# Attention values with the value block as the stationary side, SiLU gates from tanh, and weight splits in halves, in a two-layer decoder trunk

## What is computed

```python
h = rmsnorm(x, norm_even[i])
proj = h @ w_in_even[i]
(qa, ka, va, ga, qi, ki, wi, qb, kb, vb, gb, lr) = _split(proj, EVEN_SPLIT)
o_a = dsa_attention(qa, ka, va, qi, ki, wi, rel_bias, top_k)   # top 128 keys of each query
#   logits = einsum('bqhd,bqkhd->bhqk', qa, ks) * scale + bias
#   p = softmax(logits);  return einsum('bhqk,bqkhd->bqhd', p, vs)
o_a = o_a.reshape(B, S, A_W) * jax.nn.silu(ga)
...
o_b = gla(qb, kb, vb, log_a)
o_b = rmsnorm of each head * gla_norm * jax.nn.silu(gb)
x = x + jnp.concatenate([o_a, o_b], axis=-1) @ w_out_even[i]
```

## Time and profile before

| | us |
|---|---|
| median of 3 runs | 527.7 |
| lowest, highest | 527.25, 528.91 |
| the profiled execution | 527.31 |
| its span, first to last instruction | 525.6 |

### The profile page before, as it was taken

One profiled execution on the slowest core, in us unless ns is written; L12 is line 12 of the kernel. 1 busy time (PEld: TensorE's weight loads), 2 busy tenths in 40 slices (PEclk: granted clock), 3 DMA queues, 4 the chain that ended last, 5 costly groups with the idle time before them and its releaser, 6 DMA issues.

```text
span 525.6 us, 7516 instructions
## 1 busy us (share of the span) xinstructions
PE 513.8 (98%) x2807; PEld 414.5 (79%) x2807; DVE 371.1 (71%) x770; ACT 238.8 (45%) x374; POOL 292.3 (56%) x180
## 2 busy tenths in 40 slices
PE   7999999999999999999999999999999999999994
PEld 6866888788888888788888889778777677787883
DVE  3795599669957446466451074999989999869824
ACT  6734743233220434734541445456555554167413
POOL 5470755735634175655333317599999997351701
PEclk9999999999999999999999999999999999999998
DMA  8443363222222002200445303502322222402004
GB/s 267 125 140 120 121 199 122 85 76 81 81 80 82 1 1 80 82 0 1 153 169 153 88 0 120 161 25 81 88 85 75 71 64 89 148 0 82 1 0 160
DMA packets 42386, 46.75 MB, mean 89 GB/s; under 512 B 3176, under 2 KB 30851, under 8 KB 42350
## 3 DMA queue, kind: packets, MB, share of 16 engines
q1 hardware_dynamic: 42350, 46.28, 27.8%
HBM read 44.03 MB, written 2.12 MB: 88 GB/s over the span
## 4 chain that ended last, share of the span: by engine, by line
PE 83%; DVE 10%; ACT 3%; issue 1%; DMA 1%; POOL 1%; SPq 0%; POOLq 0%; ACTq 0%; DVEq 0%
PE bank L1508 31%; PE bank L1528 29%; PE bank L1816 3%; PE bank L1726 3%; PE bank L1653 3%; DVE r_va L1071 2%; PE bank L1703 2%; DVE top L1069 2%; PE bank L1804 2%; PE bank L1715 2%; DVE r_ob L1055 1%; PE bank L1822 1%; PE bank L1544 1%; DMA w_raw<-in_w_in_even_dram 1%; PE bank L1592 1%
## 5 line engine op out<-in xcount | busy, mean ns | idle before, releaser
L536 POOL TENSOR_TENSOR w_lo<-w_raw,w_hi 128x2048 fp32r<-128x2048 f32 (+1 forms) x31 | 140.4, 4531 | 101.8 <-ACT w_hi L683 100.8
L1508 PE MATMUL bank<-hT_hi,w_hi 128*128 128x512 f32 (+1 forms) x280 | 112.9, 403 | 0.0
L1508 PE MATMUL bank<-hT_hi,w_lo 128*128 128x512 f32 (+1 forms) x280 | 110.6, 395 | 0.0
L1508 PE MATMUL bank<-hT_lo,w_hi 128*128 128x512 f32 (+1 forms) x280 | 110.5, 395 | 0.0
L1528 PE MATMUL bank<-w_hi,hT_hi 128*128 128x512 f32 x252 | 102.0, 405 | 0.1
L1528 PE MATMUL bank<-w_hi,hT_lo 128*128 128x512 f32 x252 | 98.4, 391 | 0.0
L1528 PE MATMUL bank<-w_lo,hT_hi 128*128 128x512 f32 x252 | 98.3, 390 | 0.0
L683 ACT ACTIVATE w_hi<-w_raw 128x2048 fp32r<-128x2048 f32 (+1 forms) x35 | 65.6, 1878 | 40.1 <-PE bank L1528 35.3
L1325 DVE SCALAR_TENSOR_TENSOR bank<-r_va,pvec,bank 128x512 f32<-128x512 f32 x108 | 76.0, 749 | 0.9
L616 POOL TENSOR_TENSOR r_g<-r_g 128x512 f32<-128x512 f32 x48 | 62.0, 1293 | 11.4 <-ACT r_g L869 5.7
L1508 PEld LDWEIGHTS bank<-hT_lo,w_hi 128*128 128x128 f32 (+1 forms) x280 | 52.3, 187 | 13.9 <-issue 3.4
(11 more groups left out here) (232 smaller groups left out, 787.6 us busy)
## 6 DMA issues: line engine op xcount, KB each, us to landing
w_raw<-in_w_in_even_dram SPq DMA_DIRECT2D x14, 1024.0 KB, 5.2
w_raw<-in_w_in_odd_dram SPq DMA_DIRECT2D x16, 512.0 KB, 4.6
w_raw<-in_w_out_even_dram SPq DMA_DIRECT2D x4, 1024.0 KB, 7.8
w_raw<-in_w_in_odd_dram SPq DMA_DIRECT2D x4, 1024.0 KB, 5.1
w_raw<-in_w_out_odd_dram SPq DMA_DIRECT2D x4, 1024.0 KB, 5.1
r_x<-in_x_dram SPq DMA_DIRECT2D x4, 512.0 KB, 6.0
r_x<-bias_rows SPq DMA_DIRECT2D x4, 512.0 KB, 6.0
r_x<-in_x_dram SPq DMA_DIRECT2D x1, 2048.0 KB, 8.0
```

What stands on the lines that cost most here:

```text
L536: nc.gpsimd.tensor_tensor(v(w_lo[j % 3]), v(w_raw[j % 2]), v(w_hi[j % 3]).bitcast(F32), ALU.subtract).then_inc(lo_ready, 1)
L1508: ins = nc.tensor.matmul(proj_bank(g)[0:m, :], w[:, k, P * i:P * i + m], h[:, k, :], start=(n == 0), stop=(n == 3 * KC - 1))
```

## The change

- **Values.** `pv_two_heads(p)` serves heads 2p and 2p+1 of step pair p. Now the value block (128 keys x 64) is the stationary side and the transposed probabilities (128 columns) move. The two heads write the lower and the upper 64 partitions of bank 7, so the result comes out transposed, [head pair x 64, query]. It is done at every even step, behind T(n). There are four `probT` buffers instead of two, the new ones in `r_att`.
- **Softmax sums and gates.** `empty_oa` only copies bank 7 to `oaT`. The reciprocal sums are multiplied into the gate rows of ga (`gate_by_sums`), the gate rows are transposed in place of `oa`, and the transposed gate is multiplied by `oaT` in the bank (`gated_transposed`).
- **SiLU** is x/2 (1 + tanh(x/2)): for each bank ScalarE writes x/2 and tanh(x/2) (`half_and_tanh`), VectorE multiplies (`gate_row`, at steps 12, 14, 16, 18 for gb; for ga at 28, 30 and twice behind the last step).
- **Split in halves.** In slots 12 to 15 the high part of slot s+2 is made in two halves, behind `soft(8k+3)` and behind `soft(8k+5)`, and not in one piece ahead of `soft(8k+2)`.

```diff
-        probT = [r_g[:, 2048 + 512 * i:2560 + 512 * i] for i in (0, 1)]
+        probT = [r_g[:, 2048 + 512 * i:2560 + 512 * i] for i in (0, 1)] + \
+            [r_att[:, 512 * i:512 * i + 512] for i in (0, 1)]
+        tanh_row = [r_att[:, 1024 + 512 * i:1536 + 512 * i] for i in (0, 1)]
+        oaT = r_oa[:].rearrange("p (c t) -> p c t", c=4)
...
+            def mixed_high(n, c):
+                if c < 4:
+                    act.wait_ge(gated_T, c + 1)
+                else:
+                    act.wait_ge(hT_in_bank, R_MIX + n + 1)
+                nc.scalar.activation(hT_hi[:, c, :], bank[mixed_bank(n)][:], ACT.Copy,
+                                     scale=1.0 if c < 4 else pb3[:, 2:3]).then_inc(hT_hi_ready, 1)
...
+            def half_hi(j, half):
+                if half == 0:
+                    act.wait_ge(raw_in[j % 2], raw_full[j])
+                    wait_slot_used(act, j - 3)
+                cols = slice(1024 * half, 1024 * half + 1024)
+                ins = nc.scalar.activation(w_hi[j % 3][:, cols], w_raw[j % 2][:, cols], ACT.Copy)
+                if half:
+                    ins.then_inc(hi_ready, 1)
+            def half_and_tanh(g, dst, n):
+                act.wait_ge(group_done, g + 1)
+                nc.scalar.activation(dst, proj_bank(g)[:], ACT.Copy, scale=0.5)
+                if n < 2:
+                    act.wait_ge(ob_summed, TB)
+                else:
+                    act.wait_ge(gate_rows, n - 1)
+                nc.scalar.activation(tanh_row[n % 2], proj_bank(g)[:], ACT.Tanh, scale=0.5).then_inc(act_emptied, 1)
             for s_ in range(S_OE):
-                if s_ != 2:
+                if s_ != 2 and s_ < ATT_S0:
                     split_hi(s_ + 2)
...
+                        if u < 2:
+                            half_hi(s_ + 2, u)
                         if s_ == S_GB + 1:
                             if u == 0:
                                 act.wait_ge(fill_done, len(FILLS))
-                            empty(g + u, gate_b[:, u, :])
-                        if s_ == S_GA + 1 and u < TB - 1:
-                            empty(g + u, gate_a[:, u, :])
-                    if s_ == S_GB + 1:
-                        act.wait_ge(act_emptied, evacs_through(FIRST[S_GB] + 3, "act"))
-                        nc.scalar.activation(r_vb[:], r_vb[:], ACT.Silu).then_inc(gates_silu, 1)
-            act.wait_ge(act_emptied, evacs_through(FIRST[S_GA] + 2, "act"))
-            nc.scalar.activation(gate_a[:, 0:TB - 1, :], gate_a[:, 0:TB - 1, :], ACT.Silu).then_inc(gates_silu, 1)
-            empty(FIRST[S_GA] + TB - 1, gate_a[:, TB - 1, :], func=ACT.Silu)
+                            half_and_tanh(g + u, gate_b[:, u, :], u)
+                        if s_ == S_GA + 1:
+                            half_and_tanh(g + u, gate_a[:, u, :], TB + u)
             wait_slot_used(act, S_OE - 1)
-            hT_high(R_MIX, B_FIRST, mixed_bank, lambda c: 1.0 if c < 4 else pb3[:, 2:3])
+            for n, c in enumerate(B_FIRST):
+                mixed_high(n, c)
 
             def row_squares(base, n0, half, squared=lambda t: None, rows=range(TB)):
...
+            def gated_transposed(n, c):
+                dve.wait_ge(hT_in_bank, R_MIX + n + 1)
+                dve.wait_ge(oa_emptied, TB)
+                b = bank[mixed_bank(n)][:]
+                nc.vector.tensor_tensor(b, b, oaT[:, c, :], ALU.mult).then_inc(gated_T, 1)
...
             def empty_oa(tb):
-                dve.wait_ge(pv_done, AH * (tb + 1))
-                link(nc.vector.reciprocal(row_inv[:, AH * tb:AH * tb + AH], row_sum[:, AH * tb:AH * tb + AH]))
-                inv = row_inv[:, AH * tb:AH * tb + AH].unsqueeze(2).to_broadcast([P, AH, AD])
-                nc.vector.tensor_tensor(oa[:, tb, :].rearrange("p (h d) -> p h d", h=AH),
-                                        bank[7][:].rearrange("p (h d) -> p h d", h=AH), inv,
-                                        ALU.mult).then_inc(oa_emptied, 1)
+                dve.wait_ge(pv_done, AH // 2 * (tb + 1))
+                nc.vector.tensor_copy(oaT[:, :, P * tb:P * tb + P],
+                                      bank[7][:].rearrange("p (c q) -> p c q", c=4)).then_inc(oa_emptied, 1)
+            def gate_row(row, g, n):
+                dve.wait_ge(act_emptied, evacs_through(g, "act"))
+                nc.vector.scalar_tensor_tensor(out=row, in0=tanh_row[n % 2], scalar=1.0, in1=row, op0=ALU.add,
+                                               op1=ALU.mult).then_inc(gate_rows, 1)
+            def gate_by_sums(t):
+                gate_row(gate_a[:, t, :], FIRST[S_GA] + t, TB + t)
+                h0, h1 = AH * t, AH * t + AH
+                dve.wait_ge(prob_ready, h1)
+                link(nc.vector.reciprocal(row_inv[:, h0:h1], row_sum[:, h0:h1]))
+                dve.wait_ge(gate_rows, TB + t + 1)
+                row = gate_a[:, t, :].rearrange("p (h d) -> p h d", h=AH)
+                inv = row_inv[:, h0:h1].unsqueeze(2).to_broadcast([P, AH, AD])
+                nc.vector.tensor_tensor(row, row, inv, ALU.mult).then_inc(mixed_a, 1)
...
+                if n >= 4:
+                    dve.wait_ge(pv_done, n // 2 - 1)
+                nc.vector.tensor_copy(probT[n % 4][:, 0:w], bank[6][:, 0:w]).then_inc(probT_ready, 1)
                 if n % AH == 0 and n:
                     empty_oa(n // AH - 1)
                 if n < TB:
...
                 if n == TB:
                     dve.wait_ge(ob_summed, TB)
                     nc.vector.tensor_scalar(stat[:], stat[:], 1.0 / DV, EPS, ALU.mult, ALU.add).then_inc(ob_var, 1)
+                if n in (12, 14, 16, 18):
+                    t = (n - 12) // 2
+                    gate_row(gate_b[:, t, :], FIRST[S_GB] + t, t)
+                if n in (28, 30):
+                    gate_by_sums((n - 28) // 2)
                 if n in range(20, 20 + TB):
                     t = n - 20
-                    dve.wait_ge(gates_silu, 1)
+                    dve.wait_ge(gate_rows, t + 1)
                     nc.vector.tensor_tensor(ob[:, t, :], ob[:, t, :], gate_b[:, t, :], ALU.mult).then_inc(mixed_b, 1)
                 if n in range(10, 10 + TB):
...
                     link(nc.vector.tensor_tensor(heads, heads, rstd[:, BH * t:BH * t + BH].unsqueeze(2).to_broadcast(
                         [P, BH, DV]), ALU.mult))
-            dve.wait_ge(gates_silu, 2)
-            dve.wait_ge(oa_emptied, TB - 1)
-            nc.vector.tensor_tensor(oa[:, 0:TB - 1, :], oa[:, 0:TB - 1, :], gate_a[:, 0:TB - 1, :],
-                                    ALU.mult).then_inc(mixed_a, 1)
+            gate_by_sums(2)
+            gate_by_sums(3)
+            for n in range(2):
+                mixed_low(n, B_FIRST[n])
             empty_oa(TB - 1)
-            dve.wait_ge(oa_emptied, TB)
-            dve.wait_ge(act_emptied, evacs_through(FIRST[S_GA] + TB - 1, "act"))
-            nc.vector.tensor_tensor(oa[:, TB - 1, :], oa[:, TB - 1, :], gate_a[:, TB - 1, :],
-                                    ALU.mult).then_inc(mixed_a, 1)
-            hT_low(R_MIX, B_FIRST, mixed_bank, lambda c: 1.0 if c < 4 else pb3[:, 2:3])
+            for n in range(2, 4):
+                mixed_low(n, B_FIRST[n])
+            for n in range(4, KC):
+                gated_transposed(n, B_FIRST[n])
+                if n > 4:
+                    mixed_low(n - 1, B_FIRST[n - 1])
+            mixed_low(KC - 1, B_FIRST[KC - 1])
 
...
-            def pv(n):
-                tb, h = divmod(n, AH)
-                pe.wait_ge(probT_ready, n + 1)
-                if n == 0:
+            def pv_two_heads(p):
+                tb, c = divmod(p, AH // 2)
+                pe.wait_ge(probT_ready, 2 * p + 2)
+                if p == 0:
                     pe.wait_ge(act_emptied, evacs_through(FIRST[S_VA] + 3, "act"))
-                if h == 0 and tb:
+                if c == 0 and tb:
                     pe.wait_ge(oa_emptied, tb)
                 for i in range(tb + 1):
-                    ins = nc.tensor.matmul(bank[7][:, AD * h:AD * h + AD], probT[n % 2][:, P * i:P * i + P],
-                                           va[:, i, AD * h:AD * h + AD], start=(i == 0), stop=(i == tb))
+                    for r in range(2):
+                        h = 2 * c + r
+                        ins = nc.tensor.matmul(bank[7][AD * r:AD * r + AD, P * c:P * c + P],
+                                               va[:, i, AD * h:AD * h + AD],
+                                               probT[(2 * p + r) % 4][:, P * i:P * i + P],
+                                               start=(i == 0), stop=(i == tb), skip_group_check=True)
                 ins.then_inc(pv_done, 1)
             def attend(n):
                 prob_transpose(n)
-                if n:
-                    pv(n - 1)
+                if n % 2 == 0 and n:
+                    pv_two_heads(n // 2 - 1)
...
             attend(NSTEP - 1)
-            pv(NSTEP - 1)
-
-            pe.wait_ge(act_emptied, evacs_through(FIRST[S_OE] - 1, "act"))
```

(27 more changed lines are left out.)

31 lines of the change are left out of this document (8 added, 23 removed).

## The result

The changed kernel takes **537.64 us** (median of four executions: 535.33, 536.86, 538.42 and 538.61) against 527.6 for the kernel before (527.25 to 528.91): a ratio of 1.0177, 95% interval 1.0155 to 1.0199. It is slower by 1.8%. The forecast was 537.7, the range 531 to 541.5. The median hit the number, but not for the reasons in the sum alone, as the profile shows at once: the profiled execution is the quickest of the four, 535.33 us with a span of 533.6, which is 8.0 above the profiled 527.31 of before. The sum said 10.0. So two questions follow: which terms were 2 us too large, and what adds 1.5 to 3.3 us to the three other executions.

A forecast was written before the change was run, and what follows sets the result against it. TensorE's queue was taken to bound attention. Terms of -1.1, -0.2, +1.3, +3.65, +2.3, +1.9 and +2.15 sum to +10.0 on the profiled 527.31, so 537.3, or 537.7 us by the median; range 531 to 541.5.

The forecast's parts named there:

- Bound and mechanism: TensorE's queue sets attention's time; the halves close a chain through GpSimd's first quarter and open holes on TensorE.
- Values and tanh: In attention: values of two heads side by side save 2.6 us, gates by tanh without table loads save 0.2.
- slot 13: From Y = T(11): T(13) 0.35 late, pair behind it waits for gate row, scaling and logits(15); +3.65 us.
- slot 12: T(5) 0.2 late, its pair 0.35; GpSimd's power behind later quarters makes T(7) 0.55 late, its pair 0.2; +1.3 us.
- slot 14: From Z = T(19): T(21) 0.4 late, gating of ob waits for a quarter, pair at Z+7.95; +2.3 us.
- slot 15, T(30) from X = T(27): VectorE's gate_by_sums(0) among three GpSimd quarters delays logits 31 and copy 29; T(30) at X+11.25, +1.9 us.
- tail, projection from T0 = T(30): Last transposes wait for VectorE's final copy out of bank 7; projection at T0+9.4 instead of T0+7.25, +2.15 us.
- The lock: VectorE operations with two SBUF inputs wait for GpSimd at the shared port, ending 0.55 us after a quarter.
- rival 1: Chain exists, but VectorE's added operations don't queue behind GpSimd; slot 15 costs nothing; +5.3, 533.0 us; chance 0.24.
- rival 3: No time lost in attention, ScalarE and GpSimd run further ahead; -0.45, 527.3 us, no change; chance 0.11.
- The clock: Rival: TensorE's clock falls in holes of 2 to 3 us, costing 2.8 to 5.5 more; 541 us; chance 0.08.
- Rival 4, faster: No lost time, column tiles cost no edge, pairs save half of 17.2 us; 521, smaller form 525; chance 0.09.

The follow-up runs named there:

- e1: Changed kernel with the high part in slots 12 to 15 made whole again at its old place; 526.75 us, ratio 0.9982.
- e6: Kernel of e1 with the last copy out of bank 7 made by ScalarE in place of VectorE; 525.01 us, ratio 0.995.
- e5: Changed kernel with VectorE's four gate rows one step later, at steps 13, 15, 17 and 19; 535.47 us, ratio 1.0154.
- e7: Changed kernel with the last copy out of bank 7 made by ScalarE in place of VectorE; 536.15 us, ratio 1.0162.
- e3: Changed kernel with the values of a pair's two heads one after the other instead of alternating; 539.42 us, ratio 1.0213.
- e9: Changed kernel, halves kept, with the edits of e5 and e7 and the first gate by sums moved from step 28 to 30; 531.44 us, ratio 1.0087.
- e4: Changed kernel with unused bf16 matmuls filling TensorE's holes, 36 behind T(13) and 44 before T(30); 535.63 us, ratio 1.0149.
- e2: Kernel before with only the high part in halves, behind the exponentials of heads 8k+3 and 8k+5; 531.26 us, ratio 1.006.

## Why the prediction was right, and where it was not

**Bound and mechanism: right.** TensorE's queue has no hole in e1 before the tail, and each hole of the changed kernel stands where the prediction put it; only the 0.2 us before T(5) and the 0.2 behind T(7) did not appear. Its marks all appeared: values in twos, GpSimd idle until the half releases its quarter, holes behind T(13), before T(30) and before the last transposes. Undoing the halves took away every one but those before the last transposes (e1).

**Values and tanh, -2.8: right**, -2.57 at T(31) in e1 with the last pair of values still to come, and -2.98 at the projection in e6 (263.77 against 266.75), whose tail no longer waits. No run parts the two terms.

**The halves, by slot.** Measured as after minus e1, the growth from T(12) to T(20) for slot 13 and so on, beside the sum's term:

| term | predicted | measured |
|---|---|---|
| slot 12 | +1.3 | +1.16 |
| slot 13 | +3.65 | +2.96 |
| slot 14 | +2.3 | +1.82 |
| slot 15, T(30) from X = T(27) | X + 11.25 | X + 11.11 |
| tail, projection from T0 = T(30) | T0 + 9.4 | T0 + 8.65 |

Slot 13 was mis-sized in two steps that offset each other in part. T(13) was put at Y + 5.2 and stood at 5.67 (211.86 less T(11) at 206.19); the pair behind it was put at Y + 8.6 and stood at 8.29, so that its own wait was 2.2 and not 3.1. And the 0.2 for steps 14 to 18 did not come. Slot 14 erred alike, Z + 7.95 against 7.68 (237.56 less 229.88), and 0.05 in place of 0.25 later. In the tail I had VectorE's two-source operations at 0.65 and 0.7; undisturbed by GpSimd, whose last one ends at 265.49, they follow each other at 0.60, so the copy out of bank 7 began at T0 + 7.5 (273.44) and not at 8.1, and TensorE idled 0.18 and 1.37 us where I had 1.0 and 1.5. Together these are the 2.2 us by which the sum was high: T(27) +4.68 where the terms give +5.95, then 1.75 to T(30) in place of 1.9, and 1.40 in place of 2.15.

**The lock: right.** The gate row ended 0.55 us after the quarter, as the one scaling in the earlier trace rows did, so rival 1, 533.0, is out, and rival 3, no lost time, by the holes. The Trainium skill (SBUF — State Buffer, SBUF: two separate sides) makes the shared port a lock that a VectorE operation with two SBUF inputs takes as well; the trace agrees for scalar_tensor_tensor, which no row of before had shown, and for masked biases as the other side. The rival's size for slot 15, nothing, is out by the 1.32 and 1.55 us that the two operations of `gate_by_sums(0)` took beside the quarters. e5 shows that the wait had its full price only where logits were queued behind it.

**The clock: a chance of 0.08 for something that three of four executions show.** I priced the fall at 2.8 to 5.5 us and made it an alternative to the forecast instead of adding it. Where it can be read it costs 1.56 us (e7), and it comes to some executions and not others; by their granted clocks, three of the four had it once or twice. The earlier trace rows showed one stretch at 0.87 and no hole inside attention, so the trace of before could not say how often it would fall. That the long holes bring falls is shown in the profiled executions of e3 and e7; that they are what lifts the changed kernel's median is not shown. For it: e1 and the kernel before never show two steps in 34 executions, the changed kernel does in two of four. Against it: e9 has two steps in one execution with no hole over 1.12 us in attention, and a fall at 464 to 480 us, seen in e5 and e6 behind a busy TensorE, looks the same in a time. e4's median of 535.6 points to the holes too, but within what four executions can do by themselves.

**So the agreement to 0.1 us was luck in part**: a sum about 2 too large, and a median about 2.3 above the execution that the sum describes.

**Rival 4, faster,** had the right condition: with the waits gone, the kernel is faster (525.0 in e6), though by its smaller form: 525 was put for it. The values as a whole saved some 2.8 of 17.2 us, a sixth and not half.

## What to carry to other kernels

When a step on one engine is moved behind another stage's work, follow what its result releases: here 1 us of ScalarE's copy, moved four heads later, became a wait of GpSimd for 6.5 us and 3.8 us on TensorE by itself (e2), and 9 us together with new operations in VectorE's queue. An operation of VectorE with two sources in SBUF, placed in front of the one that TensorE waited for, cost 1.4 us here, more than its own length; one step later in the same queue it cost nothing. And a gain on the bounding engine can be lost in the tail: the pairs' 2.6 us became 1.3 until one copy went to the idle ScalarE.

## What the runs showed of the hardware that I had not expected

- Behind an idle stretch of 2.2 us TensorE's clock fell in some executions of the same work and not in others (granted share 1.00 in the changed kernel and 0.57 in e7, over the same 216 to 220 us); the fall in e7 cost 1.56 us. It also fell with TensorE all but busy before it (0.50 at 476 to 478 us in e5, 0.52 at 466 to 468 us in e6).
- The wait of VectorE and GpSimd for each other goes both ways: bias 16 took 1.37 us from 212.04, with the gate row beside it until 212.64, where the next of the same shape took 0.92 at 214.50; and the scaling then ended 0.55 behind that bias.
- Eight value records taken half by half of TensorE's columns, four and four, were as long as eight in alternating halves, 0.66 us; twelve and sixteen took 1.3 and 1.45 times as long.
